# HGRN's forget strips by seven block products, the last queries' scores in four column groups, the forget rows in a free bank

## The reference, cut to what matters

```python
# first block, attention: the last 16 of 272 queries attend over all keys
s = jnp.einsum("bqhd,bkhd->bhqk", qb, k[:, :end]) * scale
s = s + F[:, :, start:end, None] - F[:, :, None, :end]    # F = cumsum(log_sigmoid(f_logit + b_forget))

# second block, HGRN branch (8 heads of 128), f has two directions of 1024 columns
qh = hd(jax.nn.silu(q))
logf = log(lb + (1 - lb) * sigmoid(f));  k = (1 - lb) * sigmoid(-f)
S_t = diag(f_t) S_{t-1} + k_t v_t^T;     o_t = S_t^T q_t
# the latents' scan takes the tokens column-major (a permutation); the contexts' as they are
```

## Time and profile before

| | before |
|---|---|
| median of 3 runs | 2009.99 us (2008.95 to 2010.81) |
| profiled execution, its own time | 2010.2 us |
| its span | 2008.5 us |
| busy: PE, PEld, DVE, ACT, POOL | 1982.1, 1781.1, 1218.0, 559.3, 176.6 us |
| recurrence (1397.6 to 1677.7 us): PE, DVE, ACT, POOL busy | 280.1, 128.9, 86.3, 0 us |
| granted clock of PE, mean | 0.997 |

### The profile page before, as it was taken

The page is one execution under the profiler, slowest core; times in us unless marked ns, Lnnn a source line. Parts: engine busy times, 40 slices in busy tenths (PEclk is TensorE's granted clock), DMA queues, the critical chain, the costliest instruction groups (busy, mean ns, idle before and its releaser), DMA issues.

```text
span 2008.5 us, 31183 instructions
## 1 busy us (share of the span) xinstructions
PE 1982.1 (99%) x12535; PEld 1781.1 (89%) x12535; DVE 1218.0 (61%) x2492; ACT 559.3 (28%) x1338; POOL 176.6 (9%) x235
## 2 busy tenths in 40 slices
PE   9999999999999999999999999999999999999998
PEld 7878999977799998888888878888888889989998
DVE  5425987572388866899668555333334555766664
ACT  3343332224533322111110032222232323232212
POOL 5110340312013200000000001000000000000000
PEclk9999999999999999999999999999999999999999
DMA  6254554343544543555553644322222224545552
GB/s 194 91 178 143 167 175 159 107 148 112 169 156 159 178 137 105 168 168 168 168 183 100 197 120 138 100 84 85 84 64 63 65 68 142 168 137 179 168 174 79
DMA packets 274873, 273.61 MB, mean 136 GB/s; under 512 B 11022, under 2 KB 272378, under 8 KB 274730
## 3 DMA queue, kind: packets, MB, share of 16 engines
q1 hardware_dynamic: 272920, 267.65, 41.9%
q0 software_dynamic: 1216, 3.32, 0.5%
q10 hardware_dynamic: 594, 0.65, 0.1%
HBM read 270.38 MB, written 1.08 MB: 135 GB/s over the span
## 4 chain that ended last, share of the span: by engine, by line
PE 95%; DVE 3%; ACT 1%; DMA 1%; issue 1%; DVEq 0%; SPq 0%; ACTq 0%
PE bank L791 51%; PE bank L1263 11%; PE bank L778 8%; PE bank L1442 6%; PE bank L920 3%; PE bank L1456 2%; PE bank L1507 1%; PE bank L985 1%; PE bank L1428 1%; PE bank L1035 1%; PE bank L1469 1%; PE bank L994 1%; PE bank L1174 1%; PE bank L1180 1%; DMA W<-in_w_out_dram 0%
## 5 line engine op out<-in xcount | busy, mean ns | idle before, releaser
L791 PE MATMUL bank<-arena,SQ 128*128 128x136 f32 (+2 forms) x2176 | 341.4, 308 | 0.4 <-ACT arena L1804 0.4
L791 PEld LDWEIGHTS bank<-arena,SQ 128*128 128x128 f32 x2176 | 307.0, 191 | 17.6 <-ACT arena L1804 0.6
L791 PE MATMUL bank<-arena,W 128*128 128x136 f32 (+2 forms) x1824 | 272.6, 301 | 2.7 <-issue 2.1
L791 PEld LDWEIGHTS bank<-arena,W 128*128 128x128 f32 x1824 | 247.6, 191 | 15.3 <-issue 4.1
L1804 ACT ACTIVATE H<-bank 128x128 f32<-128x128 f32 (+1 forms) x260 | 82.5, 317 | 536.8 <-PE bank L791 536.8
L791 PE MATMUL bank<-U,W 128*128 128x136 f32 (+2 forms) x1296 | 194.6, 303 | 0.0
L791 PEld LDWEIGHTS bank<-U,W 128*128 128x128 f32 x1296 | 176.4, 191 | 11.0 <-issue 2.9
L778 PE MATMUL bank<-U,W 128*128 128x272 f32 (+2 forms) x608 | 140.6, 392 | 2.4 <-issue 1.7
L778 PEld LDWEIGHTS bank<-U,W 128*128 128x128 f32 (+1 forms) x608 | 111.7, 185 | 29.9 <-issue 3.9
L2862 DVE SCALAR_TENSOR_TENSOR W<-W,CC 128x256 f32<-128x256 f32 x280 | 128.3, 483 | 7.0
L791 PE MATMUL bank<-arena 128*128 128x136 f32 (+1 forms) x1024 | 124.1, 278 | 0.0
(11 more groups left out here) (432 smaller groups left out, 3005.4 us busy)
## 6 DMA issues: line engine op xcount, KB each, us to landing
W<-in_ffn_w_up_dram SPq DMA_DIRECT2D x44, 1024.0 KB, 5.1
W<-in_ffn_w_in_dram SPq DMA_DIRECT2D x44, 1024.0 KB, 5.1
W<-in_ada_w_dram SPq DMA_DIRECT2D x36, 1024.0 KB, 7.1
W<-in_mix_w_in_dram SPq DMA_DIRECT2D x36, 1024.0 KB, 5.3
W<-in_w_in_dram SPq DMA_DIRECT2D x22, 1024.0 KB, 5.5
W<-in_ffn_w_down_dram SPq DMA_DIRECT2D x16, 1408.0 KB, 6.6
W<-in_ffn_w_out_dram SPq DMA_DIRECT2D x16, 1408.0 KB, 6.4
W<-in_w_out_dram SPq DMA_DIRECT2D x8, 1024.0 KB, 8.2
```

Source lines behind the costliest of these rows:

```text
L791: last = mm(o, a(k), b[:, k], start=not adds and k == 0, stop=k == kt - 1, skip_group_check=True)
```

## The change

Three things. **The recurrence's forget strips** are formed by seven products of four matmuls (28 instead of 32), the blocks being input halves by column halves, and input halves by (permuted latents, contexts). The four weight sums come from POOL, one after the other, into `WSR` (rows 8 and 9 of the slots, one set for all strips, so each sum also waits for a product of the strip before it). The token sums `TBR` come from DVE in the memory stage's second pair. A strip uses two banks, x and y, each with a near and a far half, and four copies by ACT (`kept`). DVE adds up (`fold`), and the sigmoids read the sums from SBUF (`forget`). Forget strips move to slots 0 and 1 and the queries to slot 2, whose banks are 0 and 1 as well; queries come last in a pair's weave, and before the first pair half of them comes first; `WEAVE` is rewritten so that nothing is left after L1553 but one step in the last pair. The merge's token sums move to the end of the last pair. The last memory pair's copy of `columns` moves behind the first forget strip. **The last queries' scores** use 32 of the 128 columns per head, in four column groups. **The forget rows** go to bank 4.

```diff
-WEAVE = dict(pre=10, diag=6, lev=8, ctx=10, av=10, om=12)
-WEAVE_LAST = dict(pre=8, diag=4, lev=6, ctx=8, av=6, om=6)
+WEAVE = dict(pre=14, diag=6, lev=(8, 8, 8, 8, 12, 8, 8, 8), ctx=12, av=4)
+WEAVE_LAST = dict(pre=13, diag=4, lev=(6,) * 8, ctx=8, av=6)
...
-                load(0, strip(w_mix, i * SW + R_Q))
-                load(1, strip(w_mix, i * SW + R_F))
-                load(2, strip(w_mix, i * SW + (R_F + D)))
+                load(0, strip(w_mix, i * SW + R_F))
+                load(1, strip(w_mix, i * SW + (R_F + D)))
+                load(2, strip(w_mix, i * SW + R_Q))
...
-                for j in range(HEADS):
-                    last = mm(bank[6][:, 0:T1], QC[:, j, :], KA[:, j, :], start=j == 0, stop=j == HEADS - 1)
+                for odd in range(2):
+                    for pair in range(HEADS // 2):
+                        rows, j = slice(32 * pair, 32 * pair + 32), 2 * pair + odd
+                        last = mm(bank[6][rows, 0:T1], QC[:, j, rows], KA[:, j, :], start=odd == 0, stop=odd == 1, skip_group_check=True)
...
+                take(bx)
+                for k in range(4):
+                    add(bank[bx][:, near], raw(0, 0, k), permuted_and_context(0, 0)[:, k], k, True)
+                    yield
+                take(by)
...
+                eng.wait_ge(S.wsum, p.next(S.wsum))
+                for k in range(4):
+                    add(bank[by][:, near], WSR[0][:, k], TBR[0][:, k], k, True)
+                    yield
+                eng.wait_ge(S.snap, p.next(S.snap))
...
             p.leave("recurrence")
-            weave(steps_q(0), None)
+            places["sums"] = (p.now(S.prod), p.now(S.wsum))
+            queries = steps_q(2)
+            weave(queries, 8)
+            weave(steps_f(0, True), None)
             columns()
-            for steps in (steps_f(1), steps_f(2)):
-                weave(steps, None)
+            weave(steps_f(1), None)
+            weave(queries, None)
...
+                for o, x, y, op, used in ((0, part(1, 0), part(1, 1), ALU.add, 2), (1, WSR[0], part(0, 0), ALU.subtract, 2),
+                                          (3, part(0, 1), WSR[1], ALU.subtract, 1), (2, part(0, 0), part(1, 0), ALU.subtract, 1)):
+                    if n:
+                        eng.wait_ge(S.prod, p.next(S.prod, used))
+                    eng.tensor_tensor(WSR[o], x, y, op).then_inc(S.wsum, p.inc(S.wsum))
...
+                if i == 1:
+                    token_sums(permuted_and_context, TBR)
...
+            def forget_rows():
+
+                eng.wait_ge(S.land[3], p.next(S.land[3], 16))
+                take(4)
+                for kk in range(KD):
+                    eng.wait_ge(S.us, p.now(S.us) - (KD - 1 - kk))
+                    last = mm(bank[4][0:HEADS, 0:T1], W[3][:, kk, 0:HEADS], u1(kk), start=kk == 0, stop=kk == KD - 1)
...
+            def kept(d, which):
+
+                bx = 2 * d
+                x, z, y = bank[bx][:, 0:SEQ], bank[bx + 1][:, 0:SEQ], bank[bx + 1][:, SEQ:2 * SEQ]
+                for n in which:
+                    eng.wait_ge(S.prod, p.next(S.prod, 2 if n == 2 else 1))
+                    i, src = ((0, x), (3, z), (1, x), (2, y))[n]
+                    act(SNR[d][i], src, ACT.Copy).then_inc(S.snap, p.inc(S.snap))
...
             p.meet("recurrence")
+            query(0, 0)
+            kept(0, range(4))
+            head_columns(PAIRS - 1)
+            kept(1, (0,))
...
+                    if more and lev == 2:
+                        kept(0, (0,))
+                    if more and lev == 3:
+                        kept(0, (1,))
+                    if more and lev == 4:
+                        kept(0, (2,))
+                    if more and lev == 5:
+                        kept(0, (3,))
+                        kept(1, (0,))
...
                 eng.wait_ge(S.o_full, p.next(S.o_full))
                 act(OSQ, bank[6][:, :], ACT.Square).then_inc(S.osq, p.inc(S.osq))
                 if more:
-                    forget(i + 1, 1, 0)
+                    query(i + 1, 1)
...
+            def fold(i, d):
+
+                bx = 2 * d
+                by = bx + 1
+                F = FF_[i % 2][:, d]
+                eng.wait_ge(S.snap, p.next(S.snap, 4))
+                tt(F[:, 0, SEQ:2 * SEQ], SNR[d][1], bank[by][:, 0:SEQ], ALU.add).then_inc(S.order_dve, p.inc(S.order_dve))
+                eng.wait_ge(S.order_dve, p.now(S.order_dve))
+                eng.sem_inc(S.free[by], 1)
+                eng.wait_ge(S.prod, p.next(S.prod, 6))
+                tt(F[:, 0, 0:SEQ], SNR[d][0], bank[bx][:, SEQ:2 * SEQ], ALU.add).then_inc(S.f_raw, p.inc(S.f_raw))
+                tt(F[:, 1, :].rearrange("p (a b) -> p a b", a=2), SN_LATE, bank[bx][:, 0:SEQ].unsqueeze(1).to_broadcast([P, 2, SEQ]),
+                   ALU.add).then_inc(S.f_raw, p.inc(S.f_raw))
...
+                    if more and lev == 4:
+                        fold(i + 1, 0)
```

More of the change, by code:

```diff
@@ L226, in __init__ @@
         self.sig = new("sig")
+        self.f_raw = new("f_raw")
         self.fk = new("fk")
@@ L1841, in _ @@
                 act(AG[:, :, :], AG[:, :, :], ACT.Sigmoid).then_inc(S.gate, p.inc(S.gate))
-                tile(3, 0, lambda b: act(FX[0:HEADS, :], b[0:HEADS, 0:T1], ACT.Identity, bias=PLs[l][0:HEADS, C_BF:C_BF + 1]), tiles=1)
+                eng.wait_ge(S.done[3], p.next(S.done[3]))
+                act(FX[0:HEADS, :], bank[4][0:HEADS, 0:T1], ACT.Identity, bias=PLs[l][0:HEADS, C_BF:C_BF + 1]).then_inc(S.order_act, p.inc(S.order_act))
+                eng.wait_ge(S.order_act, p.now(S.order_act))
+                eng.sem_inc(S.free[4], 1)
                 tables(LOG_EXP)
@@ L2209, in gate, with head_columns @@
                 eng.sem_inc(S.free[2 + t], 1)
+            def head_columns(i):
+                eng.wait_ge(S.mt_full, p.next(S.mt_full))
+                for h in range(2):
+                    ins = act(HMT[:, i * 2 + h, :], bank[4][:, h * SEQ:(h + 1) * SEQ], ACT.Copy, scale=col(B_ML + h, i * 2))
+                ins.then_inc(S.order_act, p.inc(S.order_act))
+                eng.wait_ge(S.order_act, p.now(S.order_act))
+                eng.sem_inc(S.free[4], 1)
             tables(LOG_EXP)
@@ L2231, in _ @@
                     gate(i, t)
-                tables(LOG_EXP)
                 if i + 1 < PAIRS:
+                    tables(LOG_EXP)
                     for h in range(2):
                         exps(h)
-                eng.wait_ge(S.mt_full, p.next(S.mt_full))
-                for h in range(2):
-                    ins = act(HMT[:, i * 2 + h, :], bank[4][:, h * SEQ:(h + 1) * SEQ], ACT.Copy, scale=col(B_ML + h, i * 2))
-                ins.then_inc(S.order_act, p.inc(S.order_act))
-                eng.wait_ge(S.order_act, p.now(S.order_act))
-                eng.sem_inc(S.free[4], 1)
+                    head_columns(i)
             def query(i, t):
-                sem = S.done[0] if t else S.half[0]
+                sem = S.done[2] if t else S.half[2]
                 eng.wait_ge(sem, p.next(sem))
@@ L2306, in _ @@
                     lookup(i, lev)
-                    if more and lev > 4:
-                        query(i + 1, lev - 5)
-                if more:
-                    forget(i + 1, 0, 0)
+                    if more and lev == 2:
[7 more added lines that the diff above has]
+                        kept(1, (0,))
+                if more:
+                    eng.wait_ge(S.f_raw, p.now(S.f_raw) + 2)
+                    kept(1, (1,))
+                    for t in range(2):
+                        forget(i + 1, 0, t)
+                    kept(1, (2,))
                 else:
@@ L2319, in _ @@
                 if more:
-                    forget(i + 1, 0, 1)
+                    kept(1, (3,))
+                    for t in range(2):
+                        forget(i + 1, 1, t)
                 else:
@@ L2329, in _ @@
                 eng.sem_inc(S.free[7], 1)
+                if more:
+                    query(i + 1, 0)
                 eng.wait_ge(S.o_full, p.next(S.o_full))
@@ L3210, in _ @@
             p.meet("recurrence")
-            token_sums(latent_tokens, TBU)
+            p.skip(S.wsum, 4 * 2 * PAIRS)
             eng.wait_ge(S.hib, p.next(S.hib, 16))
-            eng.wait_ge(S.hq, p.next(S.hq, 2))
-            for d in range(2):
-                for t in range(2):
-                    gates(0, d, t)
+            fold(0, 0)
+            for t in range(2):
+                gates(0, 0, t)
+            fold(0, 1)
+            for t in range(2):
+                gates(0, 1, t)
             for i in range(PAIRS):
```

135 lines of the change are left out of this document (90 added, 45 removed).

## The result

The changed kernel took 1998.38 us (median of four runs, 1997.89 to 2001.94), the kernel before, run beside it, 2010.40. It is faster by 12.0 us on the medians (0.6%); over all runs the ratio is 0.9946 with a 95% interval of 0.9934 to 0.9959. The forecast was 1995.5 with a range of 1991.5 to 2001.0. The profiled execution has a span of 1996.0 against 2008.5.

What follows compares the result with a forecast made beforehand. PE, busy 99% of the span, was taken to bound the kernel. Savings of 19.9 us less waits of 4.1 and 1.1 made -14.7, so 2010.2 became 1995.5 us, with a range of 1991.5 to 2001.

Steps and rivals of the forecast that it cites:

- The forget strips: Recurrence: each of 8 strips drops from 32 to 28 matmuls, saving 13.8 us; a middle pair takes 61.2.
- The scores' own time: Last queries' scores, two layers: four overlapping column groups take 1.07 us instead of 3.67, saving 5.2 in all.
- The merge: Start of the merge: PE waits for ACT's copy ahead of the fourth product, 1.1 us lost, bounds 0 and 1.5.
- Joints and levels: Recurrence pairs: joint slack of 0.7 us (0.3 for the last) and no late copy or fold at levels; cost nothing.
- The rule on a drain at each table switch: Joints of pairs: the skill's drain of about 1380 ns per switch would cost PE 2.5 us, giving 1998.0; not adopted.
- Start of the recurrence: Before the first forget product: PE waits for bank 0 until ACT reads the queries, 4.1 us lost, bounds 0 and 4.5.
- The forget rows: Layer 1: bank 4 lets them begin sooner, the fifth needing the fifth scaled block; gain 0.9 us, between 0 and 1.2.
- rival E: Recurrence levels: POOL's sums hold up DVE until PE waits, slower than before, up to 2016 us; chance 0.03.
- Single sums: Recurrence: POOL's four sums per strip, at most 1.44 us each, stay under DVE's 2.4 of slack; nothing reaches PE.
- B: Starts of recurrence and merge: PE waits at neither, 1990.3 us; chance 0.07.
- C: Recurrence: small waits at joints or levels, 1 to 2 us in each of three pairs, 1998.5 to 2001.5; chance 0.25.
- D: Layers' scores: the column groups run one after the other, as slow as today, 2000.7 us; chance 0.05.

Runs made afterwards that it cites:

- the mended one: Changed kernel with the first pair's forget strips on swapped banks, whole queries ahead of them, and the table load behind the merge's first copies: 1991.83 us.

## Why the prediction was right, and where it was off

*Right as forecast.* The forget strips: a middle pair of 61.19 against 61.2. The scores' own time: 1.05 against 1.07. The wait at the recurrence: 4.25 against 4.1, behind the chain of table load, two gates and query that was named. The merge: 1.04 against 1.1. Joints and levels: no wait of PE in the first three pairs. The rule on a drain at each table switch, which would have made 1998.0, lands near the measured time, but by none of its waits: PE waits at no diagonal, and the load of 1395.49 + 1.28 is followed by an activation at 1396.78. A total that fits is no evidence for the terms inside it.

*The step that failed* is the term "Start of the recurrence", 4.1 us lost with bounds of 0 and 4.5. It prices idle time at its own length. The wait has a second price, the half clock behind it: 1.8 to 3.1 us in the five profiled executions that have the wait (24 records in 6.9 to 8.3 us instead of 5.2), and nothing in the four in which it was filled or taken away. With it the place costs 6.8 us, above the upper bound of 4.5. It is the largest part of what is missing between 14.7 us forecast and 12.5 measured in the spans. The other parts are 0.7 of small differences, 0.4 of the scores, and 0.3 of the wait's own length and the forget rows. Against them stand 1.6 us by which the start of the program and the memory stage happened to be shorter, and these the change did not bring: without that luck the time would lie further from the forecast. The Trainium skill (TensorE: Matmul & The Clock Gate, "What's actually happening") has the rule: the clock follows "how busy the PE has been recently". By that rule, the trace agrees, a forecast wait of PE had to be priced above its length. The rows shown ahead of the prediction held a granted clock of 1.00 only, because I had looked at it in the middle of the recurrence and nowhere behind a wait; the windows of before at 1187 to 1191 would have shown it.

*Mis-sized:* the scores, 5.2 forecast, 4.8 in the trace. The row of L979 was read as having "the change to the groups and back included"; the trace shows 0.1 more on the group ahead of the scores and 0.1 more on the one behind. The forget rows come near their term, 0.9 forecast and 0.75 in the trace, with the fifth scaled block as the limit that was named, but the medians have 0.1.

*Priced too low:* rival E. That each sum "has at least 5 us until it is needed" is beside the point: PE does not wait for a sum, not even for a doubled one. What runs out is DVE's slack in the levels. Rival E put the turning point at more than 2.4 us of sums on one level's chain, "two in a row", and the doubled sums, 2.6 us, are just that: the condition was right. But by its own sum it would have cost 0.2 us there, and PE waited 1.66 and then 0.9 more for ACT, 3.4 per pair in all. Single sums stay on the safe side, as forecast.

*The rivals.* B (no wait at the starts) is wrong for this kernel and yet gives the time of the mended one within 2 us: 1990.3 forecast, 1991.8 measured. C's time, 1998.5 or more, is nearly the measured one, but its mechanism isn't there: the pairs show nothing beyond one gap of 0.3 in the last. D and E did not come.

## What to carry to other kernels

Where a change leaves PE idle on its path for some us, add what the clock costs behind it, and look at the granted clock in windows there, not at the mean of the span (0.998 here). A wait for a bank that one engine frees late is often mended by taking another bank first: a swap of two strips for one pair was worth half as much as the whole change. And in this kernel a sum moved to POOL was free only as long as DVE had slack at the very place where they met; a run with twice the sums shows how near the edge is. A row that is taken for the price of another shape needs the rows ahead of it and behind it too.

## What was not expected of the hardware

The fall of the clock isn't the same in every execution. In the memory stage PE is idle for 0.6 and 1.8 us within 3 us. In 9 of the 11 profiled executions that have these waits the clock was at 0.50 behind them for 3 to 7 us, in 2 (the changed kernel's first and the one with the scores alone) it stayed at 1.00. At the program's start it fell in 8 of 12, behind a wait of 1.6 to 1.9. Where a kernel has several such places, its time has a spread of some us that no edit explains: the changed kernel's four runs had spans of 1996.0 to 1996.7 at mean clocks of 0.997 and 0.998, and 2000.1 at 0.994. What decides between the two outcomes I did not find out.

A half clock costs less than its length suggests where another engine sets the pace: in the memory stage 6 to 7 us of it cost 1.5.

The copies on ACT run under the table that is there: with the load moved behind them the first starts at 1669.96, 0.12 behind the gates, without a load of its own, and during the load itself (from 1672.67) PE has no wait.
